# End of the even layer: GpSimd's wide multiplications issued on VectorE, weight pieces issued earlier, state steps as multiply-adds

## The chip, the cores and the metric

One Trainium2 chip, of which the program uses one core. A core has TensorE (PE, matrix products into the eight PSUM banks), VectorE (DVE), ScalarE (ACT), GpSimd (POOL) and SyncE (SP, which here only issues transfers). The engines run at the same time and meet only at semaphores. The metric is the device time of one execution in microseconds.

## The reference, cut to what matters

The program is one inference step of a two-layer decoder for a prompt of 256 positions and 8 samples of one position each; together T = 264 columns. The even layer's mixer has two head groups of 8 heads: the gated delta rule ("gdn") and HGRN2 ("hgrn"). The end of this layer computes, for HGRN2 over chunks of 32 positions:

```
Bc = jnp.cumsum(logf, axis=-2)
att = einsum(q * exp(Bc - ref), k * exp(ref - Bc))      # causal part kept
o_intra = einsum(att, v)
q_in = q * jnp.exp(Bc);  k_out = k * jnp.exp(Bc[..., -1:, :] - Bc);  f_last = jnp.exp(Bc[..., -1, :])
def step(S, xs):
    o = oi + jnp.einsum('bhck,bhkv->bhcv', q_c, S)
    S = S * fl[..., None] + jnp.einsum('bhck,bhcv->bhkv', k_c, v_c)
```

Both groups' outputs are normalised per head, multiplied by a gate and go through one output projection. Each of the 8 samples has a state of its own that takes one step.

## The kernel before

Every matrix is laid out with 128 features on the partitions. `make_plan` writes one fixed list of keys; each key is one PSUM bank's worth of TensorE work, and key number n lies in bank n mod 8. TensorE works through the list in that order, and before it writes a bank it waits until the key 8 places earlier has been drained (`drained`). Everything else is straight code on each engine in the order written; nothing is scheduled.

The stretch that the change touches follows the recurrence of the delta rule. On TensorE its order is: tiles 12 to 15 of the projection `ev_in_b`, with ("sT","gdn") after tile 12 and the sums ("hn","gdn",0..3) of the four chunks of the delta rule's head norm after tiles 13, 14, 15 and once more; then ("sO","hgrn"), the samples' outputs from their states; the turning of keys and values, ("htk",t) and ("htv",t), by transposes; the chunk products ("att",g); eight state increments ("kv",k); ("sT","hgrn"); the outputs ("ho",g) in two halves t = 0, 1; then the output projection `ev_out` with the HGRN2 head norm between its first tiles.

Tiles 5 to 15 of `ev_in_b` are multiplied from split weights. ScalarE copies a half tile of 512 columns rounded (`pieces_high`, four buffers), VectorE subtracts it from the weight (`pieces_low`), and TensorE waits for the second. The copy of a half waits until TensorE has left the half four places earlier.

ScalarE also takes four wide exponentials (`qx`, `kx`, `qin`, `ko`, 128x1024 each), takes the tiles out of PSUM with `in_b`, squares chunks for the head norm (`hn_square`), turns the sums into 1/root by Ln and Exp in pairs (`hn_roots`), and copies htk and htv out. A Silu and a Ln/Exp need different tables; going from one to the other is an ACT_TABLE_LOAD. VectorE multiplies `qx` and `kx` by queries and keys, places the samples' queries (`place_queries`, two small copies), runs the gated part of the head norm (`headnorm` with `gated`), picks the samples' rows (`pick_states`, which drains ("sO", ...)), masks the chunk products into `attb`, and runs the chain of states, `SH[k+1] = SH[k]*fl + kv`, in which ("ho", t) waits for ("kv", 4t+2). GpSimd multiplies `ko` and `qin` by keys and queries, decays the samples' states (`shs`) and writes the spread values `hws2`. TensorE's transposes wait for GpSimd's two products (`hg_pool`, 3).

Of the kernel before, what the change touches and what calls it, by code (L numbers as in the profile page):

```python
# [26 lines left out]
L = 256  # L27
NS = 8
# [271 lines left out]
def build(nc, A):  # L300
# [20 lines left out]
    with ExitStack() as ctx:  # L321
# [134 lines left out]
        def drained(eng, key):  # L456
            eng.wait_ge(psum_free[no[key] % NBANK], no[key] // NBANK + 1)
# [239 lines left out]
        def _(pool):  # L697
# [52 lines left out]
            for m in range(4):  # L750
                drained(pool, ("lin", "ev_in_b", m))
            pool.wait_ge(exp_ready, 4)
            pool.wait_ge(fk_ready, HC)
            nc.gpsimd.tensor_copy(fl, qin[:, :, HCK - 1::HCK]).then_inc(hg_pool, 1)
            pool.wait_ge(hg_pool, 1)
            nc.gpsimd.tensor_tensor(ko, ko, zk[:, :, 0:L], ALU.mult).then_inc(hg_pool, 1)
            nc.gpsimd.tensor_tensor(qin, qin, zq[:, :, 0:L], ALU.mult).then_inc(hg_pool, 1)
# [3 lines left out]
            nc.gpsimd.tensor_tensor(shs, shs, zf[:, :, L:T].unsqueeze(3).broadcast_to([128, HC, NS, HD]),  # L761
                                    ALU.mult).then_inc(sdec_ready, 1)
            full(pool, ("ho", G4[3]))
            drained(pool, ("lin", "ev_in_b", 11))
            nc.gpsimd.tensor_tensor(hws2, cst("i2", 64).unsqueeze(1).unsqueeze(1).broadcast_to([128, HC, NS, HD]),
                                    zi[:, :, L:T].unsqueeze(3).broadcast_to([128, HC, NS, HD]),
                                    ALU.mult).then_inc(w_ready, 1)
# [72 lines left out]
        def _(act):  # L840
# [283 lines left out]
            f(kx, d1, ACT.Exp, scale=-1.0).then_inc(exp_ready, 1)  # L1124
            f(qin, bcs, ACT.Exp).then_inc(exp_ready, 1)
            f(ko, d2, ACT.Exp).then_inc(exp_ready, 1)
# [7 lines left out]

            def last_in_b(i):
                in_b(12 + i)
                if i < 2:
                    pieces_high("ev_in_b", 14 + i)
            headnorm("gdn", HC, T, 1.0 / HD, out_rows("gdn"), last_in_b)
            for t in range(NCH):  # L1140
                copy_out(("htk", t), hkt[:, t, :], bank(("htk", t))[:, :])
                copy_out(("htv", t), hvt[:, t, :], bank(("htv", t))[:, :])
            act.wait_ge(mix_ready, HC)
# [225 lines left out]
        def _(pe):  # L1369
# [393 lines left out]
            pe.wait_ge(hg_dve, 2)  # L1763
            pe.wait_ge(hg_pool, 3)
# [27 lines left out]
            end(mm(b[:, 128:160], bd, qks.rearrange("p c s -> p (c s)")))  # L1792
            for t in range(NCH):
# [339 lines left out]
        def _(dve):  # L2133
# [423 lines left out]
            for m in range(HC):  # L2557
                drained(dve, ("lin", "ev_in_b", m))
            tt(qx, qx, zq[:, :, 0:L], ALU.mult).then_inc(hg_dve, 1)
            dve.wait_ge(fk_ready, HC)  # L2560
# [5 lines left out]
            pieces_low("ev_in_b", 14)  # L2566
            pieces_low("ev_in_b", 15)
            dve.wait_ge(zg_ready, 4)
            headnorm("gdn", HC, T, lambda i: oT[:, i, :], lambda i: col("gdn_norm"), lambda i: tmp[:, i % 2, :],
                     gated(zg, 0))  # L2570
            drained(dve, ("lin", "ev_in_b", 11))
            full(dve, ("sT", "gdn"))
            dve.wait_ge(mix_ready, HC)
            pick_states("hgrn")
            dve.wait_ge(att_zero, 1)
# [6 lines left out]
            dve.wait_ge(hg_pool, 1)  # L2582
            for k in range(8):
# [4 lines left out]
                if k:  # L2588
                    drained(dve, ("kv", k - 1))
                    step(tt(nxt, SH[k], fl[:, :, k:k + 1].broadcast_to([128, HC, HD]), ALU.mult))  # L2590
                    drain(tt(nxt, nxt, kv, ALU.add), key)
                else:
                    drain(V.tensor_copy(nxt, kv), key)
            full(dve, ("sT", "hgrn"))
# [5 lines left out]
            drain(ins, ("sT", "hgrn"))  # L2600
            headnorm("hgrn", HC, T, lambda i: oT[:, i, :], lambda i: col("hgrn_norm"), lambda i: tmp[:, i % 2, :],
# [619 lines left out]
```

## Time and profile before

| | us |
|---|---|
| median of 3 runs | 1048.42 (1047.42 to 1049.56) |
| the profiled execution's own time | 1047.55 |
| its span, first to last instruction | 1045.7 |
| PE busy | 989.4 (95%) |
| DVE busy | 714.9 (68%) |
| ACT busy | 429.5 (41%) |
| POOL busy | 105.0 (10%) |
| PE's share of the chain that ended last | 74% |

The profiled execution spends 1.85 us outside its span and lies 0.87 us under the median. All starts below are us from the span's start. A busy TensorE is not a fast one: its clock is granted at one of two levels, shown as 1.00 (2.4 GHz) or 0.50 (1.2 GHz), or a mean of the two within a stretch.

### The profile page before, as it was taken

To read this page: it belongs to the slowest core of one execution; us is meant where nothing else is said; L and a number is where in the kernel's file an instruction comes from. 1 tells how busy PE (TensorE), PEld (TensorE's weight loads), DVE (VectorE), ACT (ScalarE), POOL (GpSimd) and SP (SyncE) were. 2 spreads that over 40 slices of the span, in tenths; PEclk is the share of its full clock that TensorE was granted. 3 is DMA by queue.
4 is the path that set the end of the run, shared out by engine and by line. 5 is a ranking of instruction groups with operands and counts; after the bars stand their busy time and mean duration, and the time that the engine had idled before them with its cause. 6 is when DMAs were issued, how large, how long until landed. Compare 5 with 4: busy or idle time off the path is not lost.

```text
span 1045.7 us, 21028 instructions
## 1 busy us (share of the span) xinstructions
PE 989.4 (95%) x8388; PEld 879.3 (84%) x8388; DVE 714.9 (68%) x1530; ACT 429.5 (41%) x815; POOL 105.0 (10%) x205
## 2 busy tenths in 40 slices
PE   7997999889999999999999987798999999999996
PEld 5876988768897999999998774467899799999996
DVE  5875648763865798986657676596275579898642
ACT  3443226623664544444422113522276453434320
POOL 0010011211010021211000000001000002121100
PEclk9998999968999999999999997989999999999999
DMA  8331023522494455465546788974944555556531
GB/s 343 130 128 42 4 86 127 197 82 86 151 390 185 169 168 196 166 218 184 178 147 249 255 311 289 325 216 169 377 159 149 189 183 176 185 179 209 210 113 42
DMA packets 41571, 192.46 MB, mean 184 GB/s; under 512 B 4602, under 2 KB 5754, under 8 KB 24578
## 3 DMA queue, kind: packets, MB, share of 16 engines
q1 hardware_dynamic: 35858, 165.30, 45.3%
q0 software_dynamic: 4576, 24.25, 6.0%
q8 instruction: 67, 1.10, 0.4%
q10 hardware_dynamic: 1040, 1.57, 0.4%
q14 instruction: 30, 0.25, 0.1%
HBM read 183.75 MB, written 7.35 MB: 183 GB/s over the span
## 4 chain that ended last, share of the span: by engine, by line
PE 74%; issue 10%; DVE 7%; SPq 3%; DMA 3%; ACT 2%; POOL 0%; DVEq 0%; ACTq 0%; POOLq 0%
PE bank L1384 72%; DVE work L2138 3%; SPq L692 2%; PE bank L1387 1%; DVE work L2141 1%; DMA ring<-in_pool_v 1%; DMA ring<-in_pool_k 1%; SPq L665 1%; ACT work_r L856 1%; DVE ring_r L2138 1%; DMA x<-in_x 1%; DVE work L3041 1%; ACT work L856 0%; DVE ch L2423 0%; DVE sq L2138 0%
## 5 line engine op out<-in xcount | busy, mean ns | idle before, releaser
L1384 PE MATMUL bank<-h_r,ring_r 128*128 128x264 f32 (+1 forms) x896 | 237.7, 286 | 0.2 <-DVE ring_r L2138 0.2
L856 ACT ACTIVATE work_r<-ring 128x2048 fp32r<-128x2048 f32 (+1 forms) x60 | 125.0, 2087 | 191.7 <-PE bank L1384 191.7
L1384 PE MATMUL bank<-h_r,work_r 128*128 128x264 f32 x704 | 200.7, 285 | 0.0
L1384 PE MATMUL bank<-sq_r,work_r 128*128 128x264 f32 x704 | 199.9, 284 | 0.0
L2138 DVE TENSOR_TENSOR ring_r<-ring,work_r 128x2048 fp32r<-128x2048 f32 (+1 forms) x60 | 150.1, 2505 | 48.1 <-ACT work_r L856 48.1
L1384 PE MATMUL bank<-h,ring 128*128 128x264 f32 x720 | 170.5, 394 | 1.4 <-DMA ring<-in_od_in 1.4
L1384 PEld LDWEIGHTS bank<-h_r,ring_r 128*128 128x128 f32 x896 | 162.6, 188 | 0.9 <-issue 0.6
L1384 PEld LDWEIGHTS bank<-h,ring 128*128 128x128 f32 x720 | 137.8, 193 | 28.0 <-issue 4.2
L1384 PE MATMUL bank<-work_r,ring_r 128*128 128x264 f32 (+1 forms) x480 | 135.8, 283 | 0.0
L1384 PEld LDWEIGHTS bank<-h_r,work_r 128*128 128x128 f32 x704 | 132.2, 188 | 1.1 <-issue 0.9
L1384 PEld LDWEIGHTS bank<-sq_r,work_r 128*128 128x128 f32 x704 | 132.5, 188 | 0.1
L1384 PE MATMUL bank<-work_r 128*128 128x264 f32 x704 | 129.7, 285 | 3.0 <-DVE ring_r L2138 2.9
L1384 PEld LDWEIGHTS bank<-work_r 128*128 128x128 f32 x704 | 109.0, 188 | 4.0 <-issue 3.9
L1384 PE MATMUL bank<-work 64*64 64x64 f32 (+14 forms) x1248 | 99.6, 308 | 12.0 <-DVE work L2138 5.2
L1384 PEld LDWEIGHTS bank<-work 64*64 64x64 f32 (+7 forms) x1248 | 71.6, 167 | 33.2 <-issue 26.6
L856 ACT ACTIVATE work<-bank 128x512 f32<-128x512 f32 (+3 forms) x127 | 47.1, 426 | 110.7 <-PE bank L1384 76.4
L1384 PEld LDWEIGHTS bank<-work_r,ring_r 128*128 128x128 f32 x480 | 90.4, 188 | 0.5 <-issue 0.2
L2141 DVE SCALAR_TENSOR_TENSOR work<-work,vec 128x256 f32<-128x256 f32 x224 | 87.1, 425 | 4.4
L2138 DVE TENSOR_TENSOR work<-bank,rs 128x264 f32<-128x264 f32 (+1 forms) x85 | 36.2, 426 | 44.3 <-PE bank L1384 33.2
L1384 PE MATMUL bank<-mix_r,ring_r 128*128 128x264 f32 (+1 forms) x280 | 63.4, 291 | 0.2 <-DVE ring_r L2138 0.2
L2138 DVE TENSOR_TENSOR work<-work 128x512 f32<-128x512 f32 (+8 forms) x94 | 56.3, 636 | 7.6 <-ACT work L856 6.2
L1384 PE MATMUL bank<-mix,ring 128*128 128x264 f32 x256 | 57.6, 386 | 0.0
(285 smaller groups left out, 1350.3 us busy)
## 6 DMA issues: line engine op xcount, KB each, us to landing
ring<-in_gu SPq DMA_DIRECT2D x44, 1024.0 KB, 4.9
ring<-in_down SPq DMA_DIRECT2D x16, 1408.0 KB, 6.1
ring<-in_pool_k SPq DMA_DIRECT2D x64, 256.0 KB, 3.8
ring<-in_pool_v SPq DMA_DIRECT2D x64, 256.0 KB, 4.1
ring<-in_ev_in_a SPq DMA_DIRECT2D x8, 1024.0 KB, 6.8
ring<-in_ev_in_b SPq DMA_DIRECT2D x8, 1024.0 KB, 4.9
work<-in_cv POOLq DMA_DIRECT2D x8, 1024.0 KB, 15.6
ring<-in_od_in SPq DMA_DIRECT2D x8, 1024.0 KB, 5.0
```

What stands on the lines that cost most here:

```text
L665: return [sp.value_load(pages[0:1, at:at + 1], min_val=0, max_val=POOL_PAGES - 1) for s_ in (s0_, s0_ + 1) for at in (PAGES * s_ + 2 * b_, ...
L692: sp.dma_start(dst[:, 512 * j:512 * (j + 1)].unsqueeze(1), pool[bass.ds(page, 1)].rearrange("a p n -> p a n")).then_inc(ring_full[s % SLOT ...
L856: return nc.scalar.activation(out, in_, func, **k)
L1384: return nc.tensor.matmul(out, lhsT, rhs, start=start, stop=stop, skip_group_check=True)
L1387: return nc.tensor.transpose(out, in_, ident)
L2138: return V.tensor_tensor(out, a, b, op)
L2141: return V.scalar_tensor_tensor(out, a, s, b, op0, op1)
L3041: V.tensor_tensor_scan(gg[:, b, m, q, :], mag2[:, n:n + 1].broadcast_to([128, LS]), ta[:, b, m, q, :], 0.0, ALU.mult, ALU.add).then_inc(s5 ...
```

## The change

GpSimd loses its four wide multiplications in this stretch and keeps the copy `fl`, which now waits only for the third exponential. VectorE takes the products of `ko` and `qin` right after the pieces of tile 15, before its head norm, and the two 128x2048 multiplications (`shs`, `hws2`) after the chain of states. `pick_states("hgrn")` moves ahead of the head norm's gated part, whose heads 0, 1 come behind it and whose heads 2, 3 move behind the chain of states. A state step becomes four multiply-adds of 128x64, one for each chunk, in place of a multiplication and an addition of 128x256. ScalarE copies the pieces of tile 14 between its second and third exponential and those of tile 15 before the Silu of tile 12; the fourth exponential comes behind the samples' copy; the first `hn_roots` comes behind tile 15, the second behind the copies of htk and htv. TensorE's own order is unchanged; its transposes wait for VectorE's `ko`, and ("ho", ...) for `qin`.

```
@@ gpsimd @@
-            for m in range(4):
-                drained(pool, ("lin", "ev_in_b", m))
-            pool.wait_ge(exp_ready, 4)
-            pool.wait_ge(fk_ready, HC)
+            pool.wait_ge(exp_ready, 3)
             nc.gpsimd.tensor_copy(fl, qin[:, :, HCK - 1::HCK]).then_inc(hg_pool, 1)
-            pool.wait_ge(hg_pool, 1)
-            nc.gpsimd.tensor_tensor(ko, ko, zk[:, :, 0:L], ALU.mult).then_inc(hg_pool, 1)
-            nc.gpsimd.tensor_tensor(qin, qin, zq[:, :, 0:L], ALU.mult).then_inc(hg_pool, 1)
...
-            nc.gpsimd.tensor_tensor(shs, shs, zf[:, :, L:T].unsqueeze(3).broadcast_to([128, HC, NS, HD]),
-                                    ALU.mult).then_inc(sdec_ready, 1)
-            full(pool, ("ho", G4[3]))
-            drained(pool, ("lin", "ev_in_b", 11))
-            nc.gpsimd.tensor_tensor(hws2, cst("i2", 64).unsqueeze(1).unsqueeze(1).broadcast_to([128, HC, NS, HD]),
-                                    zi[:, :, L:T].unsqueeze(3).broadcast_to([128, HC, NS, HD]),
-                                    ALU.mult).then_inc(w_ready, 1)
@@ scalar @@
+            pieces_high("ev_in_b", 14)
             f(qin, bcs, ACT.Exp).then_inc(exp_ready, 1)
-            f(ko, d2, ACT.Exp).then_inc(exp_ready, 1)
...
             so_copy("gdn")
-            headnorm("gdn", HC, T, 1.0 / HD, out_rows("gdn"), last_in_b)
+            f(ko, d2, ACT.Exp).then_inc(exp_ready, 1)
+            rows = out_rows("gdn")
+            hn_square("gdn", 0, T, rows(0))
+            pieces_high("ev_in_b", 15)
+            in_b(12)
+            hn_square("gdn", 1, T, rows(1))
+            in_b(13)
+            hn_square("gdn", 2, T, rows(2))
+            in_b(14)
+            hn_square("gdn", 3, T, rows(3))
+            in_b(15)
+            hn_roots("gdn", 0, T, 1.0 / HD)
             for t in range(NCH):
                 copy_out(("htk", t), hkt[:, t, :], bank(("htk", t))[:, :])
                 copy_out(("htv", t), hvt[:, t, :], bank(("htv", t))[:, :])
+            hn_roots("gdn", 2, T, 1.0 / HD)
@@ tensor @@
-            pe.wait_ge(hg_dve, 2)
-            pe.wait_ge(hg_pool, 3)
+            pe.wait_ge(hg_dve, 3)
...
+            pe.wait_ge(hg_dve, 4)
@@ vector @@
+            pieces_low("ev_in_b", 14)
             dve.wait_ge(fk_ready, HC)
             tt(kx, kx, zk[:, :, 0:L], ALU.mult).then_inc(hg_dve, 1)
...
+            dve.wait_ge(exp_ready, 4)
+            tt(ko, ko, zk[:, :, 0:L], ALU.mult).then_inc(hg_dve, 1)
+            dve.wait_ge(hg_pool, 1)
+            tt(qin, qin, zq[:, :, 0:L], ALU.mult).then_inc(hg_dve, 1)
...
-                    step(tt(nxt, SH[k], fl[:, :, k:k + 1].broadcast_to([128, HC, HD]), ALU.mult))
-                    drain(tt(nxt, nxt, kv, ALU.add), key)
+                    for c in range(HC):
+                        ins = stt(nxt[:, c, :], SH[k][:, c, :], fl[:, c, k:k + 1], kv[:, c, :], ALU.mult, ALU.add)
+                    drain(ins, key)
...
+            rows_gated((2, 3))
+            dve.wait_ge(mix_ready, HC)
...
+            full(dve, ("sO", "hgrn"))
+            tt(shs, shs, bc4(zf[:, :, L:T]), ALU.mult).then_inc(sdec_ready, 1)
+            full(dve, ("ho", G4[3]))
+            tt(hws2, cst("i2", 64).unsqueeze(1).unsqueeze(1).broadcast_to([128, HC, NS, HD]), bc4(zi[:, :, L:T]),
+               ALU.mult).then_inc(w_ready, 1)
```

On ScalarE, from the second exponential (128x1024) on, before. The 128x512 rows are pieces (the first pair tile 14's, the second tile 15's), 128x264 from a bank is a tile of `ev_in_b`, `hsq` is a square of the head norm:

```order
L856 ACTIVATE work<-work 128x1024 [waits exp_ready]
L856 ACTIVATE work<-work 128x1024 x2
L856 ACTIVATE oT<-bank 64x4x8 [waits psum_full]
L856 ACTIVATE oT<-bank 64x4x8
L856 ACTIVATE hsq<-oT 128x264 [waits psum_free7]
L856 ACT_TABLE_LOAD
L856 ACTIVATE work<-bank 128x264 [waits psum_full]
L856 ACTIVATE ring_r<-ring 128x512 [waits piece_used,ring_full3]
L856 ACTIVATE ring_r<-ring 128x512 [waits psum_full]
```

The same place now:

```order
L843 ACTIVATE work<-work 128x1024 [waits exp_ready]
L843 ACTIVATE ring_r<-ring 128x512 [waits piece_used,ring_full3]
L843 ACTIVATE ring_r<-ring 128x512 [waits psum_full]
L843 ACTIVATE work<-work 128x1024
L843 ACTIVATE oT<-bank 64x4x8 [waits psum_full]
L843 ACTIVATE oT<-bank 64x4x8
L843 ACTIVATE work<-work 128x1024
L843 ACTIVATE hsq<-oT 128x264 [waits psum_free7]
L843 ACTIVATE ring_r<-ring 128x512 [waits piece_used,ring_full3]
L843 ACTIVATE ring_r<-ring 128x512 [waits psum_full]
L843 ACT_TABLE_LOAD
```

The pieces of tile 14 stand four places earlier, and tile 15's come ahead of the table load.

On VectorE, from the product of `kx` on, before; `ch` is where the samples' queries are placed, `tmp<-bank` is `pick_states`, `ring_r` are pieces:

```order
L2138 TENSOR_TENSOR work<-work 128x1024 [waits fk_ready]
L2138 TENSOR_TENSOR work<-work 128x32 x2
L2423 COPY ch<-work 64x4x8 [waits hq_ready]
L2423 COPY ch<-work 64x4x8
L2138 TENSOR_TENSOR ring_r<-ring,ring_r 128x512 [waits piece_high] x4
L2141 SCALAR_TENSOR_TENSOR tmp<-oT,vec,hr 128x264 [waits hr_ready,zg_ready]
```

Now:

```order
L2132 TENSOR_TENSOR ring_r<-ring,ring_r 128x512 [waits piece_high] x2
L2132 TENSOR_TENSOR work<-work 128x1024 [waits fk_ready]
L2132 TENSOR_TENSOR work<-work 128x32 x2
L2417 COPY ch<-work 64x4x8 [waits hq_ready]
L2417 COPY ch<-work 64x4x8
L2132 TENSOR_TENSOR ring_r<-ring,ring_r 128x512 [waits piece_high] x2
L2132 TENSOR_TENSOR work<-work 128x1024 [waits exp_ready]
L2132 TENSOR_TENSOR work<-work 128x1024 [waits hg_pool]
L2132 TENSOR_TENSOR tmp<-bank,con 128x512 [waits psum_full,psum_free4]
L2548 TENSOR_REDUCE ch<-tmp 128x64 [waits psum_free7]
```

Tile 14's subtractions stand ahead of `kx` and of the small copies; the products of `ko` and `qin` and `pick_states` come right behind tile 15's.

## Rows read from the trace of the kernel before

**Rows 1.** The chain that ended last: start, us, engine, tile, line, count.
```profile
218.45 56.62 PE bank L1384 x440
```
**Rows 2.** Timeline, GpSimd then VectorE: start, us, engine, line, operation, count.
```profile
197.67 2.34 POOL L757 TENSOR_TENSOR work<-work 128x1024 f32<-128x1024 f32 x1
...
195.44 4.60 DVE L2423 COPY ch<-work 64x32 f32<-64x32 f32 x2
```
**Rows 3.** Line L2423: ns min/median/max of one, first and last start.
```profile
L2423 DVE COPY ch<-work x4: 174/1236/2296, 88.7 to 197.8; 64x32 f32<-64x32 f32 x4
```
**Rows 4.** Timeline of TensorE; in brackets the idle before and who ended it.
```profile
193.40 0.39 PE L1384 MATMUL bank<-sq_r,ring_r 128*128 128x264 f32 x1
...
196.41 0.61 PE L1384 MATMUL bank<-hsq,con 128*128 128x264 f32 x2
...
200.92 0.36 PE L1384 MATMUL bank<-sq_r,ring_r 128*128 128x264 f32 x1 [3.90 <-DVE ring_r L2138]
...
209.76 1.06 PE L1384 MATMUL bank<-work,ch 128*32 128x512 f32 x8
210.75 1.97 PE L1387 MATMUL bank<-con,work 128*128 128x128 f32 x16
212.99 1.16 PE L1384 MATMUL bank<-work 64*128 64x128 f32 x16 [0.27 <-ACT lnb L856]
218.45 6.58 PE L1384 MATMUL bank<-work 64*128 64x128 f32 x144 [4.30 <-DVE tmp L2138]
...
226.15 12.18 PE L1384 MATMUL bank<-work 128*64 128x128 f32 x144
```
**Rows 5.** Timeline of ScalarE.
```profile
189.19 1.14 ACT L856 ACTIVATE ring_r<-ring 128x512 fp32r<-128x512 f32 x2
190.23 4.04 ACT L856 ACTIVATE work<-work 128x1024 f32<-128x1024 f32 x4
...
195.03 1.28 ACT L856 ACT_TABLE_LOAD   x1
196.32 0.39 ACT L856 ACTIVATE work<-bank 128x264 f32<-128x264 f32 x1
...
207.88 0.85 ACT L856 ACTIVATE lnb<-bank,epst 128x264 f32<-128x264 f32 x2
...
213.74 2.05 ACT L856 ACTIVATE work<-bank 128x512 f32<-128x512 f32 x4
```
**Rows 6.** Timeline of VectorE.
```profile
162.23 0.85 DVE L2141 SCALAR_TENSOR_TENSOR sg<-sg,egc,bank 128x64 f32<-128x64 f32 x4
...
186.10 2.36 DVE L2138 TENSOR_TENSOR work<-work 128x1024 f32<-128x1024 f32 x2
188.37 1.29 DVE L2138 TENSOR_TENSOR ring_r<-ring,ring_r 128x512 fp32r<-128x512 f32 x2
...
217.62 0.69 DVE L2138 TENSOR_TENSOR tmp<-bank,con 128x512 f32<-128x512 f32 x1 [0.20 <-DVE h L2138]
218.34 1.03 DVE L2554 TENSOR_REDUCE ch<-tmp 128x64 f32<-128x512 f32 x1
219.28 2.57 DVE L2579 COPY_PREDICATED work<-con,bank 128x512 f32<-128x512 int32 x4
...
222.27 0.43 DVE L2138 TENSOR_TENSOR work<-work 128x256 f32<-128x256 f32 x1
...
245.35 0.49 DVE L2141 SCALAR_TENSOR_TENSOR tmp<-oT,vec,hr 128x264 f32<-128x264 f32 x1 [15.78 <-ACT hr L856]
```
**Rows 7.** Stretches: us, busy (count) of PE, PEld, DVE, ACT, POOL; PE clock; DMA share; GB/s.
```profile
101.00:131.00 30.00, 30.00 (x981) 29.94 (x979) 17.22 (x46) 8.26 (x22) 1.19 (x3) 0.96 0.02 4
200.92:205.23 4.31, 4.31 (x24) 4.31 (x25) 1.66 (x3) 0.00 (x0) 0.00 (x0) 0.65 0.02 4
218.45:238.26 19.81, 19.81 (x294) 15.91 (x294) 10.10 (x23) 1.18 (x2) 0.00 (x0) 0.50 0.01 2
```

More of the change, by code:

```diff
@@ L1133, in _ @@
             so_copy("gdn")
[L1135 to L1138, printed above, removed]
-            headnorm("gdn", HC, T, 1.0 / HD, out_rows("gdn"), last_in_b)
+            f(ko, d2, ACT.Exp).then_inc(exp_ready, 1)
[10 more added lines that the diff above has]
+            hn_roots("gdn", 0, T, 1.0 / HD)
             for t in range(NCH):
@@ L2565, in _, with rows_gated @@
             place_queries(qfs)
-            pieces_low("ev_in_b", 14)
             pieces_low("ev_in_b", 15)
-            dve.wait_ge(zg_ready, 4)
-            headnorm("gdn", HC, T, lambda i: oT[:, i, :], lambda i: col("gdn_norm"), lambda i: tmp[:, i % 2, :],
-                     gated(zg, 0))
+            dve.wait_ge(exp_ready, 4)
+            tt(ko, ko, zk[:, :, 0:L], ALU.mult).then_inc(hg_dve, 1)
+            dve.wait_ge(hg_pool, 1)
+            tt(qin, qin, zq[:, :, 0:L], ALU.mult).then_inc(hg_dve, 1)
+            def rows_gated(heads):
+                headnorm("gdn", heads, T, lambda i: oT[:, i, :], lambda i: col("gdn_norm"), lambda i: tmp[:, i % 2, :],
+                         gated(zg, 0))
             drained(dve, ("lin", "ev_in_b", 11))
             full(dve, ("sT", "gdn"))
-            dve.wait_ge(mix_ready, HC)
             pick_states("hgrn")
+            dve.wait_ge(zg_ready, 4)
+            dve.wait_ge(picked_ready, 2)
+            rows_gated((0, 1))
             dve.wait_ge(att_zero, 1)
@@ L2581, in _ @@
                                         blocks(("att", g))), ("att", g))
-            dve.wait_ge(hg_pool, 1)
             for k in range(8):
```

## The prediction

> **What bounds the kernel now.** I read the chain of waits first. From 218.45 on it is 56.62 us of TensorE without a break [rows 1], so whatever brings the outputs ("ho") forward brings the rest forward. Then I read TensorE's own order for the holes ahead of that point [rows 4]: 3.90 us before tile 14 of `ev_in_b`, ended by VectorE's piece, and 4.30 us before the second half of the chunk products ("att"), ended by the `tmp` that drains ("sO","hgrn"). Third, the timelines of VectorE and GpSimd tell why the first hole is there: VectorE's two tiny copies of the samples' queries take 4.60 us and end at 200.04, just as GpSimd's second product ends (197.67 + 2.34 = 200.01) [rows 2]. The same line's shortest is 174 ns [rows 3]. So the copies wait for GpSimd's products, and the pieces of tile 14 stand behind the copies. Last I read the clock. After the first hole the next 4.31 us were granted 0.65. From 218.45 to 238.26 it was 0.50 throughout, although TensorE was busy the whole time [rows 7]: once lost, this stretch of short products does not lift it.
>
> **The change, tile 14 to the transposes.** Nothing that TensorE does up to the end of tile 13 at 196.41 is moved. A tile takes 196.41 − 193.40 = 3.01 us [rows 4].
>
> ScalarE, from 190.23, with 1.01 for an exponential (4.04 / 4) and 0.57 for a half piece (1.14 / 2) [rows 5]: two exponentials to 192.25, the first half of tile 14 to 192.8. The second half waits until TensorE has left tile 12, at the latest at 193.40, and ends at 194.0. Then an exponential to 195.0, the samples' copy (0.4, like the 0.39 of a tile [rows 5]) to 195.4, the last exponential to 196.4, a square to 196.8. So the first head-norm sum starts 0.4 us later than its 196.41. Tile 15's halves end at 197.9, the table load (1.28 [rows 5]) at 199.2, tile 12's copy and the second square at 200.0.
>
> VectorE, from 192.8: product of `qx` (2.36 / 2 = 1.18 [rows 6]) to 194.0, tile 14's subtractions (1.29 for two [rows 6]) to 195.3, product of `kx` to 196.5, the small ones and the two copies at 0.17 [rows 3] to 197.1, tile 15's subtractions to 198.7, `ko` to 199.9, `qin` to 201.1. The products moved here from GpSimd lie beside tiles 14 and 15. Without that cover, `ko`'s 1.2 us would stand before the transposes.
>
> TensorE: sum 0 (0.6) to 197.4, tile 14 to 200.4, sum 1 to 201.0, tile 15 to 204.0, two sums (1.0) to 205.0, the samples' outputs (210.75 − 209.76 = 0.99) to 206.0. The transposes start there instead of at 210.75 [rows 4]: 4.75 us earlier. The 3.90 of idle and the half clock behind it are gone; about 0.4 comes back at sum 0.
>
> **The transposes to the outputs.** The transposes (1.97 [rows 4]) end at 208.0. ScalarE takes tile 15 at 204.0 to 204.4, loads the table to 205.7, two Ln (0.85) to 206.5, two Exp (no longer than the Ln) to 207.3, four copies (2.05 [rows 5]) to 209.4, and only then the second pair of Ln, the first of which (0.43) frees the bank of the second "att" key at 209.8. That is a new wait of 1.8 us where there was 0.27. The products start at 209.8 instead of 212.99 [rows 4], 3.2 us earlier. Two table loads are saved, but the copies ahead of the roots eat most of that.
>
> The 4.30 goes entirely: `pick_states` drains its bank at 206.0 + 0.69 = 206.7, and with its reduction (1.03) and four operations of the head norm of about 0.45 [rows 6] VectorE is free at 209.5, before the first product is finished.
>
> From the first "att" product to the first output there are 1.16 and 226.15 − 218.45 = 7.70 us of work [rows 4], the 7.70 at half clock [rows 7]. With the same mix the outputs start at 209.8 + 8.86 = 218.7, a gain of 7.5. If the clock lasts through both halves of "att" (second half 1.16 instead of 2.32) it is 217.5 and 8.6, and about 0.5 more if it also lasts to the samples' product, 9.1. If it is lost in the 1.8 us wait, the first half doubles too: 219.8 and 6.3. The samples' square was counted late, which may return 0.4. I take 8.4, between the mix and the upper end, because the wait is less than half of either old hole.
>
> VectorE does not bind: the masks (2.57 / 4 = 0.64 each [rows 6]) end within 0.7 us of the last "att" product, 213.8 at the latest, the first state at 214.2, two more by 216.1, and the outputs need those. A step of four multiply-adds is 0.85, against two operations of 0.43 [rows 6] with a wait between them: 0 to 0.2 us a step, hidden, so I put it at nothing.
>
> The Trainium skill (VectorE: DVE Perf Modes, the section on the trn2 errata) speaks against this edit: each instruction pays a fixed cost, so more and smaller ones are dearer. By its formula, an estimate, four from PSUM cost 0.77 and the old pair 0.72, which would make the seven steps 0.3 us longer, where the row makes them no longer.
>
> **Behind the outputs.** They take 12.11 us at half clock as before [rows 7], for nothing in the change feeds them faster. The two 128x2048 multiplications on VectorE are an estimate of 2 x 1.18 each, twice the row of 1024 columns. `shs` lies under the outputs, `hws2` starts when they end and lasts 2.4. VectorE was idle for 15.78 us until the HGRN2 norm's first root, at 245.35, 7.1 us behind the end of the outputs [rows 6]; so both are hidden, and would cost up to 4.7 if that cover were gone. The gain moves through the unbroken chain of [rows 1] to the end.
>
> **Sum.** 1048.42 − 8.4 = 1040.0. In the profiled execution's terms it is a span of 1037.3 and an own time of 1039.2; that execution lay 0.87 under the median. With 6.3 to 9.7 for the clock and the square the forecast's own range is 1038.7 to 1042.1.
>
> **Rivals.**
> 1. The clock holds from tile 14 to `ev_out`. For it: from 101 to 131 TensorE ran short 64x64 products at a mean of 0.96 [rows 7], and both old holes were 3.90 and 4.30 while the new one is 1.8. Against it: the products of 32 and 64 rows from 218.45 on never lifted the clock, so they may not keep it either. Then the outputs start at about 217 and take 6.1 instead of 12.11; VectorE's seventh state, at about 219, does not stop them. Gain 9.1 + 6.0 = 15.1, or a little more from the first product of `ev_out`: about 1033. The Trainium skill (TensorE: Matmul & The Clock Gate, the section on why this matters for kernels) names long idle pauses between bursts as what loses the clock, which read alone is this case; [rows 7] show that work of a weak kind goes with a low clock too.
> 2. GpSimd is not what holds the copies, and they stay at 2.3 each. Tile 15's subtractions are then 4.3 us later, its first half at about 202.4 for a tile due at 201.0; 1.4 to 1.8 lost, 1041.8. [rows 2, 3] speak against it.
> 3. Slower: VectorE's product of `qin` now waits for GpSimd's copy `fl`, which is queued behind the transfer of `shs` and a memset. `pick_states`, the head norm, the masks and the states all stand behind that wait. It decides once `fl` ends later than about 201; past the 3 us of slack at the products each us costs one, so 11 us of gain and slack are gone from about 215 on, giving 1052 if GpSimd comes at 219. Against it: GpSimd reached its products at about 195 with four exponentials to wait for instead of three [rows 2].
> 4. The gain is given back behind the outputs by a transfer: no idle piece stands in the 56.62 [rows 1], so I give it little; 1048.
>
> **How the numbers follow.** Forecast 0.77 (1040.0), rival 1 0.12, rival 2 0.04, rival 3 0.04, rival 4 0.03. A measurement of this kernel can tell about 0.2% (2.1 us) from no change. Faster: 0.77 + 0.12 + 0.04 = 0.93; same 0.03; slower 0.04. The range takes in the forecast's own, rival 2, and 4.7 us towards rival 1 for a clock that is lost part of the way: 1034 to 1043.
>
> **What would show it.** Right: no hole before tile 14, copies of about 0.2 us, transposes about 5 us earlier, one wait of about 2 us before "att" ended by ScalarE's `lnb`, none before its second half, outputs of about 12 us at 0.50. Wrong: copies still of 2 us (rival 2), outputs of 6 to 7 us at 1.00 (rival 1), VectorE idle before `qin` (rival 3), or a new idle of TensorE behind the outputs (rival 4).

## The result, and the profile after

The changed kernel takes 1034.34 us, median of 7 runs (1029.79 to 1037.98). The kernel before, run beside it, takes 1043.6 us, median of 7 (1041.77 to 1049.56). The ratio is 0.9889, 95% interval 0.9864 to 0.9915. The forecast was 1040.0, or 0.992 of the 1048.42 it started from: the sign is right, and more was gained than the 8.4 us forecast. The ratio stands for 11.6 us of 1043.6, its interval for 8.9 to 14.2; the two medians lie 9.26 apart. The profiled execution took 1029.79, with a span of 1028.0.

Here is TensorE's timeline of the changed kernel over the stretch in question (start, us, engine, line, operation, shapes, count; in brackets the idle time before and who ended it):

```profile
187.70 1.06 PE L1378 MATMUL bank<-work,ch 128*32 128x512 f32 x8
...
195.31 0.68 PE L1378 MATMUL bank<-hsq,con 128*128 128x264 f32 x2
198.73 0.61 PE L1378 MATMUL bank<-hsq,con 128*128 128x264 f32 x2
202.08 1.05 PE L1378 MATMUL bank<-hsq,con 128*128 128x264 f32 x4
203.06 1.06 PE L1378 MATMUL bank<-work,ch 128*32 128x512 f32 x8
204.06 2.06 PE L1381 MATMUL bank<-con,work 128*128 128x128 f32 x16
207.92 4.72 PE L1378 MATMUL bank<-work 64*128 64x128 f32 x160 [1.81 <-ACT lnb L843]
212.57 0.44 PE L1378 MATMUL bank<-con,ch 128*64 128x128 f32 x4
212.94 0.41 PE L1378 MATMUL bank<-work,con 128*128 128x32 f32 x2
214.29 12.07 PE L1378 MATMUL bank<-work 128*64 128x128 f32 x144 [0.94 <-DVE work L2135]
226.28 3.89 PE L1378 MATMUL bank<-h,ring 128*128 128x264 f32 x8
```

Read against [rows 4]. The three head-norm sums now follow each other at 3.4 us: no hole is left before tile 14 or 15. The att products and the state products (kv) are one run of 160, with no hole between att's halves; in its place are two short waits, 1.81 us before att for ScalarE's `lnb` (the logarithm of the head norm's sums, which empties the banks that att needs) and 0.94 us before the first output for VectorE's states. The rows of 4 and 2 products behind the 160 are ("sT","hgrn"), called the samples' products below. The first row is the state product of the gdn recurrence, ("sO","gdn"); up to there both programs do the same work in the same order on TensorE, and I measure every kernel from its start. In the trace of before it starts here:

```profile
188.80 1.06 PE L1384 MATMUL bank<-work,ch 128*32 128x512 f32 x8
```

The first output therefore starts 214.29 − 187.70 = 26.59 us behind it, against 226.15 − 188.80 = 37.35 before: **10.76 us gained in this stretch**.

The clock by stretch (us, busy and count of PE, PEld, DVE, ACT, POOL, then the granted clock, as in [rows 7]), from the transposes to the samples' products, and then the outputs:

```profile
204.06:212.57 8.51, 6.70 (x180) 6.21 (x176) 6.83 (x14) 4.71 (x12) 0.91 (x1) 1.00 0.63 231
...
214.29:226.28 11.99, 11.99 (x144) 8.85 (x144) 8.54 (x28) 1.18 (x2) 0.56 (x1) 0.51 0.04 13
```

att and kv now run at the full 2.4 GHz (1.00); before, everything from 218.45 on was at 1.2 GHz [rows 7]. The outputs still fall to it at their very start. VectorE's two copies took 4.60 us in [rows 2]. Here they take 0.37; behind them stand tile 15's subtractions and the two products taken over from GpSimd:

```profile
195.56 0.37 DVE L2417 COPY ch<-work 64x32 f32<-64x32 f32 x2
195.95 1.29 DVE L2132 TENSOR_TENSOR ring_r<-ring,ring_r 128x512 fp32r<-128x512 f32 x2
197.16 2.35 DVE L2132 TENSOR_TENSOR work<-work 128x1024 f32<-128x1024 f32 x2
```

What lies outside. The changed kernel's profile began the stretch 1.1 us earlier (187.70 against 188.80) for reasons that lie before it; over all 14 profiles of this case the start varies from 186.15 to 190.15. From the end of the stretch the lead of 12.0 us is constant within 0.2 until a stage behind 590 us: of two rows that are the same work in both traces (before, then after), the first pair is 11.88 us apart, the second 17.73.

```profile
579.48 1.93 PE L1384 MATMUL bank<-ring,mix 128*32 128x256 f32 x32 [0.85 <-DVE mix L2844]
...
789.74 0.59 PE L1384 MATMUL bank<-hsq,con 128*128 128x256 f32 x2
```

```profile
567.60 1.93 PE L1378 MATMUL bank<-ring,mix 128*32 128x256 f32 x32 [0.84 <-DVE mix L2852]
...
772.01 0.59 PE L1378 MATMUL bank<-hsq,con 128*128 128x256 f32 x2
```

I count the 5.85 us between as chance. The change touches nothing there, and in that stage TensorE waits for transfers, for a time that differs between executions of the same program. The same wait in the changed kernel's first profile and in its second (a1_control):

```profile
622.43 3.64 PE L1378 MATMUL bank<-ring,mix 128*32 128x256 f32 x32 [2.39 <-DMA ring<-in_pool_k]
```

```profile
625.58 3.34 PE L1378 MATMUL bank<-ring,mix 128*32 128x256 f32 x32 [4.84 <-DMA ring<-in_pool_k]
```

Between the two rows lie 204.41 us in the first profile of the changed kernel and 207.60 and 206.06 in two more, whose spans are 1032.6 and 1027.2 us although their stretch is the same (below); the kernel before has 210.26, and other variants, whose edits lie elsewhere too, reach from 205.06 to 210.65. So the whole time of one execution says little about a few us, and I judge by the stretch.

### The profile page after: what moved, and what is told of

Its sections match the earlier page's. It is cut to its first block, busy times and chain, and to the rows that moved or that the text cites. A ratio compares the mean times of both kernels' runs of the same rounds, so it can differ in the third digit from the quotient of the medians.

```text
span 1028.0 us, 21036 instructions
## 1 busy us (share of the span) xinstructions
PE 979.5 (95%) x8388; PEld 871.2 (85%) x8388; DVE 716.8 (70%) x1548; ACT 427.2 (42%) x813; POOL 92.9 (9%) x201
## 4 chain that ended last, share of the span: by engine, by line
PE 75%; issue 9%; DVE 6%; SPq 3%; DMA 2%; ACT 2%; POOL 0%; DVEq 0%; ACTq 0%; POOLq 0%
PE bank L1378 74%; DVE work L2132 2%; SPq L692 2%; DVE work L2135 2%; DMA ring<-in_pool_v 1%; PE bank L1381 1%; SPq L665 1%; ACT work L843 1%; ACT work_r L843 1%; DMA x<-in_x 1%; DVE work L3049 1%; DMA ring<-in_pool_k 1%; DVE ring_r L2132 0%; DVE sq L2132 0%; ACT lnb L843 0%
## 5 line engine op out<-in xcount | busy, mean ns | idle before, releaser
L1378 PE MATMUL bank<-work 64*64 64x64 f32 (+14 forms) x1248 | 97.1, 297 | 9.4 <-DVE work L2132 5.1
L1378 PEld LDWEIGHTS bank<-work 64*64 64x64 f32 (+7 forms) x1248 | 69.2, 156 | 29.8 <-issue 24.2
L2135 DVE SCALAR_TENSOR_TENSOR work<-work,vec 128x256 f32<-128x256 f32 x224 | 84.9, 415 | 4.4
```

Source lines behind the costliest of these rows:

```text
L1378: return nc.tensor.matmul(out, lhsT, rhs, start=start, stop=stop, skip_group_check=True)
L2135: return V.scalar_tensor_tensor(out, a, s, b, op0, op1)
```

## Experiments

Of the edits only the telling lines are shown, with ... where lines are left out. All times in the table are us from the start of the state product, worked out from each profile's own rows: to the transposes, to att, to the first output (the first product of ("ho", ...)), to the first product behind the outputs (`ev_out`), and then what lies between the last two. Ratio: against the kernel before on the same chip, with its 95% interval.

| kernel | transposes | att | first output | `ev_out` | outputs | ratio |
|---|---|---|---|---|---|---|
| before | 21.95 | 24.19 | 37.35 | 49.46 | 12.11 | 1 |
| changed | 16.36 | 20.22 | 26.59 | 38.58 | 11.99 | 0.9889 [0.9864, 0.9915] |
| a1_control | 16.35 | 20.21 | 26.59 | 38.70 | 12.11 | 0.9889 [0.9854, 0.9924] |
| a2_control | 16.35 | 20.21 | 26.59 | 38.12 | 11.53 | 0.9896 [0.9868, 0.9924] |
| e1_products_on_gpsimd | 18.33 | 22.19 | 28.56 | 39.48 | 10.92 | 0.9881 [0.9847, 0.9915] |
| e2_pieces_in_place | 17.89 | 21.75 | 28.12 | 39.17 | 11.05 | 0.9904 [0.987, 0.9938] |
| e12_products_and_pieces_back | 21.95 | 25.81 | 32.19 | 43.47 | 11.28 | 0.9938 [0.9915, 0.996] |
| e3_pick_behind_norm | 16.35 | 20.22 | 30.84 | 42.95 | 12.11 | 0.9926 [0.99, 0.9951] |
| e4_two_op_states | 16.36 | 20.22 | 26.65 | 38.49 | 11.84 | 0.9881 [0.983, 0.9932] |
| e5_logs_ahead | 16.35 | 18.49 | 25.35 | 37.45 | 12.10 | 0.9871 [0.9832, 0.991] |
| e8_logs_ahead_rows_behind | 16.35 | 18.49 | 24.86 | 33.49 | 8.63, of it 1.22 idle | 0.9865 [0.9828, 0.9902] |
| e8_again | 16.36 | 18.50 | 24.87 | 36.98 | 12.11 | 0.9856 [0.9831, 0.988] |
| e9_fine_waits | 16.36 | 18.49 | 24.71 | 36.81 | 12.10 | 0.9867 [0.984, 0.9893] |
| e7_before_products_on_vector | 17.60 | 19.84 | 32.95 | 45.06 | 12.11 | 0.9961 [0.9936, 0.9986] |

**The changed kernel again** (no edit).

> The changed kernel once more, a second profile of it. From the start of the even layer's first state product (sO gdn) to the start of the recurrence's first output it took 26.59 us in the first profile, against 37.35 us in the kernel before. Both theories (the gain lies in this stretch and is the same in each execution; or the stretch varies from one execution to the next and the 10.8 us were luck): the first expects 26.4 to 26.8 us again and the granted clock at 1.00 up to the first output, whatever the whole time is; the second expects 28 us or more. Whole time 1030 to 1038 us, the spread from the stage behind 590 us.

> The changed kernel a third time, beside the two kernels built on it. First output 26.5 to 26.7 us behind the state product, and outputs of 11 to 12.2 us, as in the two profiles of it so far; whole time 0.989 of the kernel before.

The first output came at 26.59 us in all three profiles, to the hundredth. Up to there the program decides the stretch; the outputs vary by 0.6 us (11.53 to 12.11), and the spans differ elsewhere.

**The products back on GpSimd.**

```diff
+            nc.gpsimd.tensor_tensor(ko, ko, zk[:, :, 0:L], ALU.mult).then_inc(hg_pool, 1)
+            nc.gpsimd.tensor_tensor(qin, qin, zq[:, :, 0:L], ALU.mult).then_inc(hg_pool, 1)
...
-            tt(ko, ko, zk[:, :, 0:L], ALU.mult).then_inc(hg_dve, 1)
...
-            tt(qin, qin, zq[:, :, 0:L], ALU.mult).then_inc(hg_dve, 1)
```

> The changed kernel with the two wide products (ko, qin) back on GpSimd, all else as changed. Theory (GpSimd at work is what makes VectorE's two copies of pieces take 2.3 us each): the copies take about 2.3 us each again in place of 0.18, the low pieces of tile 15 come late, TensorE idles about 1 us ahead of that tile or of the transposes, and the first output starts 0.9 to 1.0 us later than 26.59 us behind the state product. Rival (the copies were held by ScalarE's own writing or by their place behind the exponentials): the copies stay at 0.2 us and the first output stays within 0.2 us.

GpSimd's two products and, under them, VectorE's:

```profile
196.41 2.38 POOL L757 TENSOR_TENSOR work<-work 128x1024 f32<-128x1024 f32 x1 [0.97 <-ACT work L850]
198.76 2.42 POOL L758 TENSOR_TENSOR work<-work 128x1024 f32<-128x1024 f32 x1
```

```profile
195.26 3.68 DVE L2140 TENSOR_TENSOR work<-work 128x1024 f32<-128x1024 f32 x3
198.98 2.43 DVE L2425 COPY ch<-work 64x32 f32<-64x32 f32 x2
```

VectorE's three operations take 3.68 us where they took 1.47, and the copies 2.43 where they took 0.37. Each group ends 0.2 us behind one of GpSimd's products (198.94 behind 198.79, 201.41 behind 201.18): in these rows a VectorE instruction that starts under such a product ends with it. TensorE waits for the result ahead of tile 15:

```profile
202.28 0.36 PE L1385 MATMUL bank<-sq_r,ring_r 128*128 128x264 f32 x1 [1.73 <-DVE ring_r L2140]
```

That is the theory's cause, but not its picture. It had both copies held; of the copies one is held (2.24 us) and the other takes 0.18, and the first GpSimd product holds one of the two small 128x32 products ahead of them instead (2.40 us in place of about 0.2). The loss is 1.97 us in place of 1.0.

**The pieces in their old places.**

```diff
-            pieces_high("ev_in_b", 14)
             f(qin, bcs, ACT.Exp).then_inc(exp_ready, 1)
...
             in_b(12)
+            pieces_high("ev_in_b", 14)
...
```

> The changed kernel with the pieces of tiles 14 and 15 written where they were written before, on ScalarE and on VectorE, all else as changed (products on VectorE). Theory (the products on GpSimd were the larger part of the hole ahead of tile 14): TensorE idles about 1.0 us there and the first output starts about 1.0 us later than 26.59 us. Rival (the early pieces are the main gain): the hole of 3.9 us is back and the first output starts 3.5 us or more later.

1.53 us later where the theory had 1.0, and far from the rival's 3.5: with the copies short, the old place of the pieces leaves a hole of 1.38 us.

**Both undone.** The two edits above together.

> The changed kernel with both undone together: the two wide products back on GpSimd and the pieces of tiles 14 and 15 in their old places; the early pick of states, the later drains and the multiply-adds stay. All theories expect the hole ahead of tile 14 back, 3 to 4.5 us. Theory (the hole also cost clock behind it, so the att and kv products ran between the two clock levels before): att, kv and what follows up to the first output take 7.5 to 9 us in place of 6.4, and the first output starts 5.5 to 7 us later than 26.59 us. Rival (the hole costs its own length and no clock; the clock before fell for another reason): att to first output stays at 6.4 us and the first output starts 3 to 4.5 us later.

The hole before tile 14 is back to the hundredth, and so are the transposes, at 21.95:

```profile
199.88 0.36 PE L1385 MATMUL bank<-sq_r,ring_r 128*128 128x264 f32 x1 [3.90 <-DVE ring_r L2140]
```

The two parts overlap: each alone loses 1.5 to 2.0, both 5.59. The first output is 5.60 later, inside the theory's range, but not by its mechanism: att to first output stayed at 32.19 − 25.81 = 6.38, as the rival had it. What clock this hole costs, it costs in the tile right behind it. The granted clock is the number behind POOL's; the second row lies inside att and kv:

```profile
200.00:206.00 6.00, 6.00 (x36) 5.93 (x37) 1.55 (x3) 0.81 (x2) 0.00 (x0) 0.72 0.01 3
...
214.00:216.00 2.00, 2.00 (x48) 1.88 (x48) 1.19 (x2) 0.43 (x2) 0.00 (x0) 1.00 0.67 231
```

Tile 14 and what follows it up to the next head-norm sum take 4.51 us (199.88 to 204.39) in place of 3.09; by att the clock is at 1.00 again. So the slow att of the kernel before must have another cause.

**The pick of the states late.**

```diff
-            pick_states("hgrn")
             dve.wait_ge(zg_ready, 4)
-            dve.wait_ge(picked_ready, 2)
             rows_gated((0, 1))
+            rows_gated((2, 3))
+            dve.wait_ge(mix_ready, HC)
+            pick_states("hgrn")
...
-            rows_gated((2, 3))
-            dve.wait_ge(mix_ready, HC)
```

With the pick, the gated rows of heads 2, 3 go back ahead of the masks, as they stood in the kernel before.

> The changed kernel with the second pick of states back behind the gated rows, where it was before, all else as changed. The banks of att's second half are then drained late, and a hole of 2.5 to 3.5 us comes back inside att (4.30 us before). Theory (it is the hole inside att that cost the clock before, since with the hole ahead of tile 14 back att to first output stayed at 6.4 us): the granted clock falls behind this hole and before the outputs, the att and kv products take 5.5 to 7.5 us of busy time in place of 4.72, and the first output starts 4.5 to 6 us later than 26.59 us behind the state product. Rival (the clock holds through a hole of this length, and before it fell for another reason): busy time stays at 4.7 us, and the first output starts 2.5 to 3.7 us later, by the hole alone.

```profile
207.30 1.16 PE L1378 MATMUL bank<-work 64*128 64x128 f32 x16 [1.81 <-ACT lnb L843]
210.57 6.22 PE L1378 MATMUL bank<-work 64*128 64x128 f32 x144 [2.11 <-DVE tmp L2132]
```

```profile
210.57:217.92 7.35, 7.35 (x151) 6.61 (x151) 6.93 (x22) 0.00 (x0) 0.00 (x0) 0.53 0.01 2
```

The same 160 products take 1.16 + 6.22 = 7.38 us in place of 4.72, at a granted clock of 0.53 behind the hole (210.57 to 217.92): here is the clock of the kernel before. The first output is 4.25 later: 2.11 of hole, 2.66 in att and kv, 0.48 in the samples' products, less the 0.94 that TensorE no longer waits for VectorE, together 4.31. The theory holds; its 4.5 was a little high because it left that last credit out. The three profiles with a hole inside att (before, e7 and this one) have a half clock behind it up to the first output; in the other eleven att and kv ran at the full one (4.72 to 4.73 us, or 2.06 and 2.74 with a wait between). Here the 1.81 us wait stands 1.16 us ahead of the hole, and no run has a hole of 2.11 without it.

The hole is only 2.11 us, though, where before it was 4.30. The rest is GpSimd again. In the trace of before, GpSimd's product over `shs` and the third gated row on VectorE:

```profile
212.14 3.63 POOL L761 TENSOR_TENSOR work<-work 128x2048 f32<-128x2048 f32 x1
```

```profile
213.57 2.50 DVE L2141 SCALAR_TENSOR_TENSOR tmp<-oT,vec,hr 128x264 f32<-128x264 f32 x1 [2.58 <-ACT hr L856]
```

The row takes 2.50 us where its neighbours take 0.49, and ends 0.30 behind GpSimd. It stood ahead of the pick, so by its length about 2.0 of the 4.30 us were this product's; no run took this product alone away. The two kernels can be compared here: in both the third row starts 0.58 to 0.59 us before TensorE stops. The prediction had put the whole hole down to the pick's place.

Not every VectorE instruction is held. Earlier in the trace of before GpSimd runs a product as wide, and VectorE works under it:

```profile
133.20 3.62 POOL L734 TENSOR_TENSOR work<-con,work 128x2048 f32<-128x2048 f32 x1
```

```profile
133.28 1.29 DVE L2138 TENSOR_TENSOR work<-bank,work 128x512 f32<-128x512 f32 x2 [0.33 <-PE bank L1384]
134.48 1.40 DVE L2470 COPY sq<-bank 64x256 f32<-64x256 f32 x4
```

These six end at 134.57 and 135.88, while GpSimd works until 136.82. They read a PSUM bank; every instruction that was held reads nothing from PSUM. The Trainium skill (GPSIMD Engine Reference, Specifications) says that GpSimd shares its interfaces to SBUF, the core's main on-chip memory, with VectorE and collides with VectorE instructions that read two inputs there or run in a two-port mode. The gated row (`oT`, `hr`) and the six agree, and the rows add the price. The held copies read one input; whether they run in that mode no run here shows. The engines of this kernel thus meet at more than semaphores.

**The step of the states by two instructions.**

```diff
-                    for c in range(HC):
-                        ins = stt(nxt[:, c, :], SH[k][:, c, :], fl[:, c, k:k + 1], kv[:, c, :], ALU.mult, ALU.add)
-                    drain(ins, key)
+                    step(tt(nxt, SH[k], fl[:, :, k:k + 1].broadcast_to([128, HC, HD]), ALU.mult))
+                    drain(tt(nxt, nxt, kv, ALU.add), key)
```

> The changed kernel with each state step as a multiplication and an addition over all four heads, as before, in place of four multiply-adds, all else as changed. Theory (VectorE sets the first output since the picks moved ahead of the masks, and a step by two instructions takes 0.98 us against 0.94): the first output starts 0.1 us later (two steps), and the whole time is the same within 0.3 us. Rival (the multiply-adds are worth something themselves, a step by two instructions costs 0.2 us or more in addition): the first output starts 0.4 us later or more. [...]

0.06 us later: the two steps that the first output waits for cost 0.98 us each in place of 0.94 (215.25 − 214.27 there, 5.65 us for six steps in the changed kernel). The multiply-adds are worth next to nothing, and are not the dearer form. The rows, of the pair there and of the six steps in the changed kernel:

```profile
214.27 0.43 DVE L2132 TENSOR_TENSOR work<-work 128x256 f32<-128x256 f32 x1
214.73 0.42 DVE L2132 TENSOR_TENSOR work<-work,bank 128x256 f32<-128x256 f32 x1
215.25 0.42 DVE L2132 TENSOR_TENSOR work<-work 128x256 f32<-128x256 f32 x1
```

```profile
212.11 5.65 DVE L2135 SCALAR_TENSOR_TENSOR work<-work,bank 128x64 f32<-128x64 f32 x24
```

The rule that the prediction took from the Trainium skill (VectorE: DVE Perf Modes, the section on the trn2 errata), by which more and smaller instructions are dearer, puts the four at 0.77 and the pair at 0.72 by the estimate there. The rows go against that order here, with 0.94 for the four and 0.98 for the pair.

**The logarithms ahead of the copies.** `hn_roots` is split in its two halves.

```diff
             hn_roots("gdn", 0, T, 1.0 / HD)
+            hn_logs("gdn", 2, T, 1.0 / HD)
             for t in range(NCH):
                 copy_out(("htk", t), hkt[:, t, :], bank(("htk", t))[:, :])
                 copy_out(("htv", t), hvt[:, t, :], bank(("htv", t))[:, :])
-            hn_roots("gdn", 2, T, 1.0 / HD)
+            hn_exps("gdn", 2, T)
```

> The changed kernel with ScalarE's second pair of logarithms, which drains the banks that att waits for, ahead of the four copies of htk and htv; the exponentials stay behind them. Theory (these copies are the whole of the 1.81 us wait ahead of att, and VectorE's masks then start behind the gated rows, 1.1 us earlier): the wait shrinks to 0.2 to 0.4 us, the kv products wait for the copies for less than 0.5 us, and the first output starts 1.0 to 1.2 us earlier than 26.59 us. Whether the clock then holds into the outputs is open: if the 1.81 us wait is what brings it down, the outputs take 6 to 9 us; if the outputs themselves bring it down, 11 to 12.2 us as now. Rival (kv waits for the copies for as long as att did before): first output within 0.2 us of 26.59 us.

1.24 us earlier, a little over the theory's 1.0 to 1.2; the wait before att is gone, and kv waits 0.38 us for the copies. The clock fell all the same, now already at the samples' products ahead of the outputs; the first four of these take 0.70 in place of 0.44:

```profile
212.09 0.70 PE L1400 MATMUL bank<-con,ch 128*64 128x128 f32 x4
```

So it falls without the 1.81 us wait as well.

**The gated rows behind the states as well.** `rows_gated((0, 1))` goes from ahead of the masks to behind the states.

> The kernel with the logarithms ahead, and all four gated rows on VectorE behind the states. Theory (VectorE's chain pick, two gated rows, masks, states is what sets the first output): the masks start as soon as the first att bank is written, 1.7 us earlier than in the changed kernel, and the first output starts 1.6 to 2.2 us earlier than 26.59 us; the output weights product behind the outputs does not wait for the rows, which end 4 us ahead of it. Rival (TensorE's own att and kv products bind as soon as the wait is gone): no more than 1.2 us, as with the logarithms alone. Slower rival: the exponentials of the second pair wait for the gated rows and hold ScalarE's output copies, and the product behind the outputs waits: later by 1 us or more at that place.

> The kernel with the logarithms ahead and the four gated rows behind the states, a second time. Reading A (the program's own order keeps the full clock through the outputs): the outputs take 7.4 us again and end 32.3 us behind the state product. Reading B (luck of the moment): the clock falls before or in the outputs, which then take 9 to 12.2 us. Whole time by A 6 us under the changed kernel's, by B 2 us.

The first output is 1.73 us earlier in the one and 1.72 in the other: VectorE's chain was what set it. The two executions differ in the outputs. The first, and the same program again:

```profile
212.20:219.60 7.40, 7.29 (x144) 5.46 (x144) 6.88 (x27) 0.85 (x2) 0.56 (x1) 1.00 0.06 21
```

```profile
211.30:223.40 12.10, 12.10 (x144) 8.95 (x144) 10.21 (x32) 2.03 (x4) 0.56 (x1) 0.50 0.04 13
```

The same 144 products, fed in the same way, took 7.4 us at 2.4 GHz once and 12.1 at 1.2 GHz the other time. Reading B is right: the full clock through the outputs is no property of the order of the program. In the first execution TensorE then waited 1.22 us for the gated rows, which the theory had 4 us ahead of it; in e8_again, with the outputs at half clock, it does not wait.

**Two finer waits.** On top of the kernel above.

```diff
-            pe.wait_ge(mix_ready, 4)
-            half_product("ev_out", 0, 0, h)
+            half_product("ev_out", 0, 0, h, lambda k: pe.wait_ge(mix_ready, k + 1))
...
-                drained(pe, ("kv", 4 * t + 2))
...
+                            if c == 0:
+                                drained(pe, ("kv", k - 1))
```

> The kernel with the logarithms ahead and the gated rows behind the states, with two waits of TensorE made finer: each group of outputs waits for the state it reads and not for the third state, and the output weights product waits for one gated row at a time and not for all four. Theory: the 0.49 us ahead of the outputs and the 1.22 us ahead of the output weights product, seen with the rows behind the states, go to 0 to 0.3 us each. On the clock two readings stand against each other. Reading A (TensorE kept busy without a pause over half a microsecond from the transposes on keeps the full clock through the outputs): the outputs take 7 to 8 us, and end 30.5 to 31.5 us behind the state product, against 38.58 in the changed kernel and 32.27 with the rows behind the states. Reading B (the full clock in that run was luck of the moment, since with the logarithms ahead alone, and pauses of the same lengths, it fell): the outputs take 11 to 12.2 us in this run, and end 35 to 36.5 us behind the state product.

The first output is 1.88 us earlier than in the changed kernel, with 0.34 us of idle before it, a little over the theory's 0.3; the clock fell at the outputs, reading B again, and they end at 36.81. At their slow pace nobody waits for the gated rows, so the second edit could not show its worth.

Are these kernels better than the changed one? In the stretch, by 1.1 to 1.9 us (36.81 and 36.98 to `ev_out` against 38.12 to 38.70), the one execution with the full clock left out. In whole time beside a2_control (mean of 6 runs 1033.86) e9_fine_waits has 1031.44 and e8_again 1030.86; their ratios to before, 0.9867 and 0.9856 against 0.9896, have intervals that overlap. Both beat the kernel before; that they beat the changed one is likely from the stretch and not shown by the times.

**The products alone, in the kernel before.** Only `ko` and `qin` go to VectorE.

> The kernel before with one part of the change alone: the two wide products (ko, qin) on VectorE behind the low pieces, in place of GpSimd. Theory (GpSimd's products hold VectorE's copies, and that is most of the hole ahead of tile 14): the hole of 3.90 us shrinks to 0 to 1.5 us, the transposes start 2.4 to 4 us earlier, the hole of 4.30 us inside att stays (its wait is for the late pick), and the first output starts 2.4 to 4 us earlier than 37.35 us behind the state product. Rival (the pieces' place is the cause): the hole stays above 3 us and the first output within 1 us of 37.35 us.

4.40 us earlier: the hole before tile 14 shrinks from 3.90 to 1.09, the transposes come 4.35 us earlier, and the hole inside att stays. The gain is a little over the theory's 4, which counted the hole and not the half clock in tile 14 behind it. The rows of att and kv are as in the kernel before:

```profile
209.99 1.16 PE L1381 MATMUL bank<-work 64*128 64x128 f32 x16 [0.26 <-ACT lnb L853]
215.40 6.58 PE L1381 MATMUL bank<-work 64*128 64x128 f32 x144 [4.25 <-DVE tmp L2134]
```

GpSimd's product over `shs` is still in this kernel, and holds the third gated row for 2.46 us as before.

## Why the prediction was right in direction and too small

The 10.76 us are made up of four terms, each from the rows of the two timelines: att starts 24.19 − 20.22 = 3.97 earlier; the hole of 4.30 is gone; the work from att to the first output takes 5.43 us (207.92 to 213.35) in place of 8.86, a gain of 3.43; and 0.94 is lost to the new wait for VectorE. 3.97 + 4.30 + 3.43 − 0.94 = 10.76. The forecast's 8.4 had 3.2 + 4.30 + 0.9 in their place. Against the prediction's steps:

- **Tile 14 to the transposes** was forecast at 4.75 and measured 5.59. The mechanism held: copies of 0.18 each, no hole, and GpSimd as the cause (e1, e7). The 0.4 for the first sum did not come: it starts 7.61 us behind the state product in both kernels, since ScalarE's square ends in time. The other 0.44 is the price of a tile with a sum, put at 3.6 and measured at 3.42 and 3.35.
- **The new wait before att** was forecast at 1.8, ended by `lnb`, and is 1.81, ended by `lnb`; e5 shows that the four copies are its whole cause.
- **The 4.30 going entirely** was right, but it was put down to the pick alone. e3 gives the pick 2.11; most of the rest was GpSimd's product over `shs`, whose removal the prediction counted as hidden work behind the outputs and nothing more. The 4.30 goes all the same because the change removes both.
- **The step that failed is the work from att to the first output.** Of the 8.4, 0.9 was left for the clock here; it is 3.43. Even its upper end allowed 0.5 + 1.16: it halved the second half of att, gave 0.5 to the samples' product, and had no term for the kv products between them. Rival 1, in which the clock holds, has the same gap: its outputs start at about 217 by the same 9.1. For kv at half clock the text gives no reason but the remark under rival 1 that such short products never lifted a clock once lost, so that they may not keep one. The runs show that they keep one: att and kv ran at 1.00 in all eleven profiles without a hole inside att. e3 prices it: 2.66 us for att and kv, 0.48 for the samples' products.
- **What held the clock back** was the hole inside att, not the one ahead of tile 14 (e12 against e3). The prediction had judged the new wait by its length beside either old hole, as if both had cost the same.
- **"VectorE does not bind"** failed: once TensorE runs att and kv at full clock it arrives 0.94 us ahead of the third state. The new wait takes back part of the clock's gain. The price of the multiply-adds at 0 to 0.2 a step was right (0.04, e4).
- **The outputs at half clock, 12.11** was right: 11.5 to 12.1 in three profiles. Rival 1 was not what happened, but e8 shows once that it can; at the full clock the outputs then took 7.40, not the 6.1 that rival 1 had by halving.
- **Behind the outputs** nothing came up: the `shs` product lies under the outputs, `hws2` under `ev_out`, and TensorE runs on. Rivals 2 to 4 did not occur: GpSimd's copy `fl` ended at 194.23, well ahead of the 201 from which rival 3 decides.
- **Two sums** that the forecast does not rest on do not come out as written: the named terms give 9.5 and not 9.7 for the upper end (9.1 and the square's 0.4), and 201 with 3 us of slack and 8.4 of gain is about 212 and not 215 in rival 3.

Most of the distance from 1040.0 to 1034.34 is the level, which says nothing of the mechanism: the kernel before ran 1043.6 here, in the median of 7, against the 1048.42 of 3 runs that the sum started from. 8.4 us off 1043.6 would be 1035.2, and the stretch's own 10.9 (`ev_out` 49.46 − 38.58) gives 1032.7; the measured median lies between the two.

## What to carry to other kernels

When GpSimd works on wide elementwise products, look on VectorE's timeline for short instructions without a PSUM operand that have long durations and end when GpSimd's do; moving GpSimd's work can be worth more than its own time, in places that have no dependence on it. When a hole in TensorE's work is removed ahead of a chain of short products, price that chain at both clocks, all of it, and ask which engine feeds it at the faster pace. Where the time of one execution varies by more than the effect, measure the stretch from an instruction that both kernels reach in the same way.

## What the runs showed of the hardware beyond that

- A hole costs clock at different places: 3.90 us before a tile of 264-column products cost it within that tile only (0.72 over 6 us in e12), and the clock was back by att; 2.11 us inside att, with short products behind it, cost it through kv and the samples' products (0.53 in e3), 3.1 us of work ahead of the outputs, where it falls anyway in 13 of the 14 profiles.
- TensorE busy without a pause at 1.2 GHz through 12 us of outputs, and the same program at 2.4 GHz in another execution (12.1 and 7.4 us): the same code has both outcomes. What tells them apart at the outputs is not settled by these runs: neither the wait of 1.81 us (e5) nor the pause ahead of the outputs (0.34 in e9, 0.94 in the changed kernel, 0.49 in the execution that kept the clock) decides it.
- A 64x32 copy on VectorE that costs 0.17 us alone was held up to 2.3, and a 128x264 gated row of 0.49 up to 2.50, each to about the end of GpSimd's instruction; under a GpSimd product of 3.62 us, VectorE instructions that read a PSUM bank kept their pace. The same price is still paid elsewhere in the changed kernel: a 128x256 multiply-add of 0.48 us takes 0.86 under GpSimd's 128x264 products, 29 times behind 350 us. What that costs the whole was not measured.
